# Gated DeltaNet in a two-layer encoder trunk: four batches prepared together, 16x16 diagonal blocks inverted on VectorE, the upper three levels on TensorE

## What is computed

```python
gc = cumsum(g); decay = where(tril, exp(gc_i - gc_j), 0)
a_mat = where(strict, (k*beta) @ k.T * decay, 0)
lhs = a_mat + eye
value = triangular_solve(lhs, v*beta)              # lower, unit diagonal
k_cumdecay = triangular_solve(lhs, k*beta*exp(gc))
qk = (q @ k.T) * decay
# over the chunks:
v_new = value - k_cumdecay @ state
out = (q*exp(gc)) @ state + qk @ v_new
state = state*exp(g_last) + (k*exp(g_last-gc)).T @ v_new
```

## Time and profile before

| | us |
|---|---|
| median of 3 runs (2016.3 to 2016.98) | 2016.49 |
| the profiled execution, its time | 2016.86 |
| the profiled execution, its span | 2015.1 |
| TensorE busy | 1926.2 |
| VectorE busy | 1499.4 |
| ScalarE busy | 1126.6 |
| GpSimd busy | 73.7 |

### The profile page before, as it was taken

The page is one execution under the profiler, slowest core; times in us unless marked ns, Lnnn a source line. Parts: engine busy times, 40 slices in busy tenths (PEclk is TensorE's granted clock), DMA queues, the critical chain, the costliest instruction groups (busy, mean ns, idle before and its releaser), DMA issues.

```text
span 2015.1 us, 27100 instructions
## 1 busy us (share of the span) xinstructions
PE 1926.2 (96%) x10976; PEld 1645.9 (82%) x10976; DVE 1499.4 (74%) x1868; ACT 1126.6 (56%) x1249; POOL 73.7 (4%) x67
## 2 busy tenths in 40 slices
PE   9988989889999997988999999999999999999998
PEld 8976868889998986767978888888888888888886
DVE  8657585565547657665588888988889888888986
ACT  5543323333334643423477777777777777777775
POOL 1002011000000001111000000000000000000000
PEclk9997889899999997988999999999999999999999
DMA  7400000545434400002489999999999999999994
GB/s 301 165 27 1 1 1 12 209 148 178 164 121 185 137 27 1 1 1 84 179 320 349 353 354 357 351 341 356 349 360 350 342 355 349 360 352 367 355 360 183
DMA packets 64196, 443.57 MB, mean 220 GB/s; under 512 B 8172, under 2 KB 8204, under 8 KB 13632
## 3 DMA queue, kind: packets, MB, share of 16 engines
q1 hardware_dynamic: 62032, 437.87, 58.2%
q0 software_dynamic: 1760, 3.78, 0.5%
q10 hardware_dynamic: 272, 0.10, 0.0%
HBM read 440.66 MB, written 2.17 MB: 220 GB/s over the span
## 4 chain that ended last, share of the span: by engine, by line
PE 88%; DVE 10%; issue 1%; ACT 0%; DMA 0%; POOL 0%; SPq 0%; DVEq 0%; POOLq 0%; ACTq 0%
PE ps L1891 23%; PE ps L1893 22%; PE ps L1892 22%; PE ps L2278 2%; PE ps L2263 2%; PE ps L2282 2%; PE ps L1904 2%; DVE cacc L1245 2%; DVE w_lo L1153 2%; PE ps L2057 1%; PE ps L2434 1%; PE ps L2445 1%; PE ps L2104 1%; PE ps L2140 1%; PE ps L2069 1%
## 5 line engine op out<-in xcount | busy, mean ns | idle before, releaser
L1210 DVE TENSOR_TENSOR m_lo<-raw,m_hi 128x2048 fp32r<-128x2048 f32 x336 | 768.4, 2290 | 135.8 <-ACT m_hi L810 135.5
L810 ACT ACTIVATE m_hi<-raw 128x2048 fp32r<-128x2048 f32 x336 | 644.1, 1918 | 268.9 <-PE ps L1893 268.9
L1891 PE MATMUL ps<-m_hi,xe_hi 128*128 128x512 f32 x896 | 358.5, 400 | 0.0
L1892 PE MATMUL ps<-m_hi,xe_lo 128*128 128x512 f32 x896 | 353.6, 395 | 0.0
L1893 PE MATMUL ps<-m_lo,xe_hi 128*128 128x512 f32 x896 | 353.6, 395 | 0.0
L1153 DVE TENSOR_TENSOR w_lo<-raw,w_hi 128x1024 fp32r<-128x1024 f32 (+1 forms) x164 | 183.6, 1155 | 126.3 <-ACT w_hi L775 126.3
L1891 PE MATMUL ps<-u_hi,w_hi 128*128 128x272 f32 x800 | 237.0, 296 | 14.7 <-DVE u_lo L1203 10.2
L1893 PE MATMUL ps<-u_lo,w_hi 128*128 128x272 f32 x800 | 233.2, 291 | 0.0
L775 ACT ACTIVATE w_hi<-raw 128x1024 fp32r<-128x1024 f32 (+1 forms) x164 | 159.7, 1002 | 129.9 <-PE ps L1893 124.5
L1892 PE MATMUL ps<-u_hi,w_lo 128*128 128x272 f32 x800 | 232.0, 290 | 0.0
L1893 PEld LDWEIGHTS ps<-m_lo,xe_hi 128*128 128x128 f32 x896 | 168.0, 187 | 41.1
(11 more groups left out here) (397 smaller groups left out, 2766.9 us busy)
## 6 DMA issues: line engine op xcount, KB each, us to landing
raw<-in_moe_units SPq DMA_DIRECT2D x336, 1024.0 KB, 4.9
raw<-in_dense_units SPq DMA_DIRECT2D x57, 1024.0 KB, 4.8
raw<-in_dense_units SPq DMA_DIRECT2D x16, 768.0 KB, 5.0
raw<-in_dense_units SPq DMA_DIRECT2D x8, 896.0 KB, 4.5
w_uq<-in_mla_w_uq SPq DMA_DIRECT2D x2, 768.0 KB, 4.4
mats<-in_c_mats POOLq DMA_DIRECT2D x1, 1216.0 KB, 10.6
h<-in_h_rows SPq DMA_DIRECT2D x2, 544.0 KB, 4.4
bias_rows<-bias_row POOLq DMA_DIRECT2D x1, 1088.0 KB, 26.4
```

What stands on the lines that cost most here:

```text
L810: nc.scalar.activation(m_hi[k % RING][:, :], raw[:, slot, :], ACT.Copy).then_inc(m_hi_ready, 1)
L1210: V.tensor_tensor(m_lo[k % RING][:, :], raw[:, mslot(k), :], m_hi[k % RING][:, :].bitcast(F32), ALU.subtract).then_inc(m_lo_ready, 1)
L1891: mm(o, w[0], x[0], start=first, stop=False)
L1892: mm(o, w[1], x[0], start=False, stop=False)
```

## The change

- All four batches get tiles of their own (`batch[s, d]`). Several lie in tiles that are free at the time: `kk` and `qk` hold X, `k_tok` holds KW, one slot of `raw` holds M. The differences take their mask as an addend (-1e30 above the diagonal) in the same instruction; gate columns of all batches come at once in `dcol`.
- Levels 0 to 3 are gone for the real tokens. The diagonal 16x16 blocks of the four batches and four heads are 128 in number, one to a partition. They are brought there by VectorE's 32x32 transposes, inverted by elementwise products and sums in steps of 2, 4 and 8, and taken back the same way into `dn_o`. TensorE transposes A for the backward direction ("ai") and the block inverses ("ot") with ScalarE's copies behind.
- Levels 4 to 6 run for all four batches side by side. The meta tokens' steps lie in the preparation.
- The products for later, the gate and beta tiles of the second pair and the masks are made on GpSimd: 30 products and one memset a layer in place of 24.
- The second output unit's load waits on SP's queue for the last X.
- Number and content of the attention turns are unchanged; where they stand changes.

```diff
-    return [("mask", s, n, d) for s in range(2) for n in range(1, LEVELS) for d in range(2)]
+    out = [("zero",), ("rows", 1, 0), ("rows", 1, 1)]
+    out += [("mask", s, BASE, d) for s, d in BATCHES] + [("pt", s, d) for s, d in BATCHES]
+    out += [("qe", 0, d) for d in range(2)] + [("mask", s, BASE + 1, d) for s, d in BATCHES]
+    out += [("vb", s, d) for d in range(2) for s in range(2)] + [("mask", s, BASE + 2, d) for s, d in BATCHES]
+    return out + [("kw", 0, d) for d in range(2)] + [("qe", 1, d) for d in range(2)]
...
-                    if u == out_units[l][2]:
+                    if u == out_units[l][1]:
+                        assert slot_of[u] == 5
...
+                        dn_pe.wait(sp, l, "x", 1, LEVELS - 1, 1)
+                    if u == out_units[l][2]:
...
+                def diff(s, d):
+                    t = (s, 1 - s)[d]
+                    pe_w("rows", s, d)
+                    for hh in range(H):
+                        i = V.scalar_tensor_tensor(batch[s, d]["DT"][:, hh], ps[:, 2 * d, P * hh:P * hh + P],
+                                                   dcol[:, 0, t, 4 * d + hh:4 * d + hh + 1], mat(M_NEG + d), ALU.subtract, ALU.add)
+                    S.mark(i, "diff", s, d)
...
+                def blocks_in():
+                    act_w("ai", 1)
+                    for q in range(4):
+                        i = V.transpose(blk[packed(q), :, :], diagonal(dn_a, q))
...
+                def blocks_level(size):
...
+                    parts = [np.s_[:, :, r] for r in range(size)] if size <= nb else [np.s_[:, b] for b in range(nb)]
+                    for at_ in parts:
+                        i = V.tensor_tensor(cube[at_], left[at_], high[at_], ALU.mult)
+                    link(i)
+                    link(V.tensor_reduce(blk_x[:, 0:nb * size ** 2], cube.rearrange("p b r c k -> p (b r c) k"), AX.X, ALU.add))
+                    for at_ in parts:
+                        i = V.tensor_tensor(cube[at_], low[at_], x_in[at_], ALU.mult)
+                    link(i)
+                    for at_ in parts:
+                        i = V.tensor_reduce(made[at_], cube[at_], AX.X, ALU.add)
+                    link(i)
+
+                def blocks_out():
+                    for b in range(2):
+                        i = V.tensor_scalar(blk_e[:, :, BLOCK * b:BLOCK * b + BLOCK], blk_u[:, :, :], pick[b], -1.0, ALU.mult, ALU.mult)
+                    link(i)
+                    dn_pool.wait(dve, l, "zero")
+                    for q in range(4):
+                        i = V.transpose(diagonal(dn_o, q), blk_e[packed(q), :, :])
+                    S.mark(i, "blocks")
...
+                meta_level(2)
+                blocks_in()
+                blocks_level(2)
+                turn_of_others()
+                blocks_level(4)
+                turn_of_others()
+                meta_level(3)
+                blocks_level(8)
+                turn_of_others()
+                blocks_out()
...
+                for n in range(BASE, LEVELS):
+                    for s in range(2):
+                        for d in range(2):
+                            B = batch[s, d]
+                            dn_pool.wait(pe, l, "mask", s, n, d)
+                            if n == BASE:
+                                act_w("ot", s, d)
+                            else:
+                                dve_w("T", s, n - 1, d)
+                            for hh in range(H):
+                                i = mm(bank_of(s, d)[:, P * hh:P * hh + P], B["M"][:, hh], B["T"][:, hh], start=True, stop=True)
+                            S.mark(i, "x", s, n, d)
+                        turn_of_others()
```

More of the change, by code:

```diff
@@ L744, in _ @@
             for l in range(DEPTH):
[L745 to L750, removed]
-                            dn_pe.wait(pool, l, "x", s, n - 1, d)
-                            level = bc(mat(M_LV + LEVELS * d + n), 1, H)
-                            dn_pool.mark(nc.gpsimd.tensor_tensor(batch[d]["M"][:, :, :], batch[d]["AT"][:, :, :], level, ALU.mult),
-                                         "mask", s, n, d)
+                S = dn_pool
@@ new lines, in _, with product, masks @@
+                S.begin(l)
+                def product(out_, in0, in1, *name):
+                    S.mark(nc.gpsimd.tensor_tensor(out_, in0, in1, ALU.mult), *name)
+                def masks(n):
+                    for s, d in BATCHES:
+                        if n == BASE:
+                            dn_dve.wait(pool, l, "prod", s, d)
+                        else:
+                            dn_pe.wait(pool, l, "x", s, n - 1, d)
+                        product(batch[s, d]["M"], batch[s, d]["AT"], bc(mat(M_LV + LEVELS * d + n), 1, H), "mask", s, n, d)
@@ new lines, in queries @@
+                def queries(s):
+                    for d in range(2):
+                        t = (s, 1 - s)[d]
+                        dn_act.wait(pool, l, "erow", s, d)
+                        product(batch[s, d]["QE"], qkv[:, 0:4, META + P * t:META + P * t + P], batch[s, d]["QE"], "qe", s, d)
+                dn_pe.wait(pool, l, "k_tok", 0)
+                S.mark(nc.gpsimd.memset(dn_o[:, :, :, :, :].rearrange("p s d h n -> p (s d h n)"), 0.0), "zero")
+                dn_dve.wait(pool, l, "gate_cols")
@@ new lines, in _ @@
+                for d in range(2):
+                    t = 1 - d
+                    nc.gpsimd.tensor_tensor(batch[1, d]["RT"], bc(mat(M_TRI + d), 1, H), bc(gcol[:, t, 0, 4 * d:4 * d + 4], 2, P), ALU.mult)
+                    product(batch[1, d]["RB"], bc(ident, 1, H), bc(gcol[:, t, 1, 4 * d:4 * d + 4], 2, P), "rows", 1, d)
+                masks(BASE)
+                for s, d in BATCHES:
+                    product(batch[s, d]["PT"], qk[:, (s, 1 - s)[d]], batch[s, d]["DT"], "pt", s, d)
+                queries(0)
@@ new lines, in _ @@
+                masks(BASE + 1)
+                for d in range(2):
+                    for s in range(2):
+                        t = (s, 1 - s)[d]
+                        product(batch[s, d]["Vb"], v_tok[:, t], bc(gcol[:, t, 1, 4 * d:4 * d + 4], 2, P), "vb", s, d)
+                masks(BASE + 2)
+                dn_act.wait(pool, l, "expcols")
+                for d in range(2):
+                    product(batch[0, d]["KW"], k_tok[:, d], bc(dcol[:, 2, d, 4 * d:4 * d + 4], 2, P), "kw", 0, d)
@@ L982, in _ @@
                 turn_of_others()
[L983 to L994, removed]
+                dve_w("m_diff")
@@ L2288, in _ @@
[L2288 to L2289 removed]
+                        else:
+                            dve_w("T", 0, LEVELS - 1, d)
                         for hh in range(H):
```

535 lines of the change are left out of this document (312 added, 223 removed).

## The result

The changed kernel took 2097.61 us (median of 4 runs, 2096.9 to 2108.22) against 2016.39 before: a ratio of 1.042, 95% interval 1.038 to 1.046. It is 81 us slower where I had forecast 51 less, outside the range and on the other side. The profiled execution took 2098.15 us with a span of 2096.4.

What follows compares the result with a forecast made beforehand. TensorE, busy 96% of the span, was taken to bound the kernel. Layer 0 saves 12.1 and 16.9 us, layer 1 9.4 and 13.1, together 51.5; from 2016.86 that gives 1965.4, forecast 1965 us, range 1938 to 1995.

Steps and rivals of the forecast that it cites:

- Second part: Levels 16 and up and the two final steps: 93.7 us in layer 0, 84.5 in layer 1, before new stalls.
- With 8 us more: 101.7 and 92.5: Second part, layers 0 and 1: adds 4 us of low clock and 4 of scores waiting for the maximum; bounds 2 and 14.
- because after it both kernels have the same turns left: Reason for cutting each layer's mixer where the 16th step of the attention work (turn 15) ends.
- Four batches side by side hide ScalarE's copies and VectorE's updates: Second part: one batch's copy takes under 1 us against 2.8 us of products of the other three.
- double turns: Second part: consecutive attention turns without DeltaNet between, scores waiting for VectorE's maximum, 0.5 to 1 us a place, 4 in all.
- First part: Mixer up to the end of turn 15: VectorE carries it, 65 + 6 + 4 = 75 us; bounds 64 and 92.
- the collisions: First part: GpSimd passes, 15 instead of 12, hold up VectorE's passes; 4 us more than the about 5 before.
- Rival 2: Clock stays low through the first part and the first level runs low: 2 x 15 back, 1995 us; chance 0.13.
- Rival 1: First part reaches 88 us from longer VectorE preparation, strided transposes and GpSimd collisions: 1991 us in all; chance 0.17.
- Rival 4: VectorE's diagonal, strided transposes are slow: beyond 3.8 us each the gain is gone, at 5 us 2036; chance 0.05.
- Rival 5: The change doesn't bind because attention turns set the pace; one costs TensorE 1.6 us; chance 0.03.
- signs of being wrong: First part above 88 us, a transpose above 1.5 us, or the clock in the levels staying below 0.9.

Runs made afterwards that it cites:

- with the turns ahead: Changed kernel with ScalarE's and VectorE's attention turns one step earlier in the levels and two final steps: 1985.86 us, 111.8 less than the changed kernel.
- the best kernel: The 1965.13 us kernel with eight X products of one level of the second pair of batches issued twice in each layer: 1956.99 us, ratio 0.972.
- the one price above: Four more GpSimd products over 128x512 a layer, on the changed kernel with attention turns moved earlier and early betas (1973 us): 1975.04 us, 2.0 more.
- one kernel: The kernel before, with only ScalarE's turn put behind its copy of X and VectorE's second turn behind its updates: 2095.17 us, ratio 1.040.
- the same kernel: The 1973 us kernel (attention turns moved earlier, early betas) with VectorE's turns ahead of parts of the inversion and one of ScalarE's ahead of its copies: 1965.13 us.

## Why the prediction was wrong

**The count of TensorE's work was right.** Second part, layer 0: 93.7 us forecast (92 without the 2 of idle time and low clock in it), 92 measured in the changed kernel and 90 (96.75 x 0.93) with the turns ahead. The 192 X products before and 96 after, in each layer, are there as forecast.

**The step that failed** is the one that reads: "With 8 us more: 101.7 and 92.5", with bounds of 2 and 14. It priced every new stall of the second part at 4 us of low clock and 4 us of scores waiting for the maximum. Measured: 169.7 us in layer 0, 76 above the 93.7, and 123.9 in layer 1, 39 above the 84.5. In layer 0 it was 32 us idle and 46 of low clock, in place of the 8. Its ground was "because after it both kernels have the same turns left" and "Four batches side by side hide ScalarE's copies and VectorE's updates". Both are true of the work and say nothing of the queue. The copies and updates were hidden; what stood behind them in the same queue was not. I had asked for one turn on one engine what it waits for (VectorE's maximum, at double turns). I did not ask it of each turn on each engine: which DeltaNet step, waiting for TensorE, stands ahead of it. Once the turns were moved, the second part took 100.0 us (forecast 101.7) in layer 0, and 82.4 in layer 1 (832.9 to 915.3, forecast 92.5).

Of the time by which the forecast was missed (133 us), the second parts hold 99 and the first parts 37; the stretches outside them were 4 shorter.

**First part: its waits were wrong, and its busy time came right by luck.** I had 69 us of VectorE with the collisions (65 + 4) and it was 70.1. But the sum starts from a wrong column: the 63.3 us that I took for VectorE are the weight loads, and the earlier trace rows has 58.9 for VectorE in layer 0 (so its room there was 28 us, not 24). From 58.9 the same terms give 60.6, and 64.6 with the collisions. What was missing is mostly the inversion: the eight transposes took 8.4 us, not 4.8, and the whole inversion, added up from the timeline, 16 in place of 11.9. GpSimd did 12 passes in the part and not 15, so the count behind the collisions was off as well; no run isolates their cost.

```profile
194.96 4.20 DVE L1663 STREAM_TRANSPOSE blk<-dn_a 32x512 f32<-32x512 f32 x4
```

Waits were 6 by forecast and 92.7 - 70.1 = 22.6 measured. I had seen that beta was "issued on TensorE behind an attention turn", and took little for it; VectorE waited 7.9 us for them, and moving them gave back 8 us in layer 0. At the end of the part, with its own work nearly done, VectorE waited 8.8 us more for TensorE (5.4, 2.6 and 0.8); the forecast has 2 to 3 for the whole chain there. In the best kernel the part still takes 82.4 us for the 75 forecast.

**The rivals.** Rival 2 named the clock, and it was 0.63 in the first part and 0.66 in the levels; but at 30 us it was too small, and in the second part the low clock came and went with the idle places. In the first part it stayed at 0.66 with the turns ahead, as this rival says; TensorE had 71.4 x 0.63 = 45 us of work there, for the 41 forecast. Rival 1 came near the length of the first part (88; it was 93), and a partly wrong reason: the transposes were longer, but the waits weighed more. Rival 4 was the only one on the side of the result: at 1.05 us a transpose it did not happen. Rival 5 had the attention turns set the pace, but by TensorE's own time for a turn (1.6 us), not by what a turn waits for. A rival "the turns stand behind steps that wait for TensorE" was missing, and with it the sign. Two of my signs of being wrong came true: a first part above 88 us, and a clock below 0.9 in the levels.

**What held:** the change as a whole does pay once its turns are moved, 1986 us against 2016; no run tells how much of it is the inversion and how much the four batches side by side. With the order of betas and first part repaired too it takes 1965 us, which is my forecast only by luck: it is another order of instructions, and the errors offset each other (first part longer, layer 1's second part shorter). With the fill it is 1957.

**Left open:** what the first part would take at the high clock (not tried), and GpSimd's share in it beyond the one price above.

## What to carry to other kernels

When work of two chains is interleaved by hand on several in-order queues, write down for each engine what stands ahead of each step and what that waits for. A step of the other chain belongs ahead of the wait on the engine that the first chain's turn comes from, or each engine idles in turn; here the order alone was worth 80 us in one kernel and 112 in the other, more than the 59 us by which the best kernel beats the one before. And read an idle place together with the granted clock behind it: in the second parts here TensorE's waits themselves were the smaller part of the price (28 of 70 us with the turns moved).

## What the hardware showed that I had not expected

An idle place of 1.09 us in a stretch where TensorE was otherwise busy was followed by groups at 1.2 GHz from 264.60 to 278 (granted clock 0.51), some 6 to 7 us lost. In layer 1 of the same kernel one of only 0.36 us was followed by some 13 us of slow groups. In the last kernel idle places of 0.81 and 0.31 us, a little later in the same stretches, were not. So the length of the idle place alone does not decide. 1.9 us of repeated products ahead of it made the kernel faster by 4 us a layer. The Trainium skill, page "TensorE: Matmul & The Clock Gate", section "What's actually happening", has the gate follow how busy TensorE has recently been; the two kernels agree with it. VectorE's transposes of 32 partitions x 512 columns took 1.05 us against 0.60 for a plain pass over as many columns.
